# A residue layout for the rows of the compressed keys and values, an immediate factor in GpSimd's rounding product, and GpSimd's loops written out

## What is computed

```python
def compress(k, pos, w1, w2):
    B, G, T, dh = k.shape
    c = k.reshape(B, G, T // CMP_STRIDE, CMP_STRIDE, dh)
    blocks = jnp.concatenate([c[:, :, :-1], c[:, :, 1:]], axis=3) + pos
    flat = blocks.reshape(B, G, blocks.shape[2], CMP_BLK * dh)
    return jax.nn.gelu(flat @ w1) @ w2
...
    kc = compress(to_g(partial_rope(kv(nkc), cos, sin)), cmp_pos_k, cmp_w1_k, cmp_w2_k)
    vc = compress(to_g(kv(nvc)), cmp_pos_v, cmp_w1_v, cmp_w2_v)
```

## Time and profile before

| | us |
|---|---|
| median of three runs | 3132.75 |
| lowest, highest run | 3125.09, 3135.55 |
| the profiled execution | 3136.32 |
| its span, from the first to the last instruction | 3134.3 |

### The profile page before, as it was taken

The page is one execution under the profiler, slowest core; times in us unless marked ns, Lnnn a source line. Parts: engine busy times, 40 slices in busy tenths (PEclk is TensorE's granted clock), DMA queues, the critical chain, the costliest instruction groups (busy, mean ns, idle before and its releaser), DMA issues.

```text
span 3134.3 us, 41325 instructions
## 1 busy us (share of the span) xinstructions
PE 3074.6 (98%) x15116; PEld 2466.4 (79%) x15116; DVE 1501.1 (48%) x2613; ACT 724.1 (23%) x1461; POOL 1902.8 (61%) x885
## 2 busy tenths in 40 slices
PE   8999999999999999999999999999999999999998
PEld 6688888868888888877688888888887668888887
DVE  4654520455552143886645455214388664545411
ACT  4410100441100123434601110012343550111000
POOL 4277778437777876001288777787700128877776
PEclk9999999999999999999999999999999999999999
DMA  3132333213333322112033333332211203233222
GB/s 124 48 108 98 97 95 100 75 34 108 101 94 95 100 87 88 48 35 81 21 94 94 101 99 95 95 100 88 87 48 35 81 22 100 94 101 94 100 94 87
DMA packets 71713, 262.29 MB, mean 84 GB/s; under 512 B 8208, under 2 KB 8208, under 8 KB 71440
## 3 DMA queue, kind: packets, MB, share of 16 engines
q1 hardware_dynamic: 71280, 258.34, 25.9%
q10 hardware_dynamic: 288, 1.98, 0.2%
HBM read 258.20 MB, written 2.10 MB: 83 GB/s over the span
## 4 chain that ended last, share of the span: by engine, by line
PE 85%; DVE 6%; issue 4%; POOL 3%; ACT 2%; DMA 0%; DVEq 0%; POOLq 0%; SPq 0%; ACTq 0%
PE bank L642 83%; POOL w_hi L1408 1%; POOL w_lo L1416 1%; PE bank L1272 1%; DVE arena L1983 1%; DVE bank L1983 1%; DVE rope L1983 1%; PE bank L657 0%; DVE arena L2354 0%; DVE rope L1980 0%; ACT act_hi L1563 0%; ACT arena L1905 0%; DVE w_lo L2380 0%; DVE x L1983 0%; ACT bank L1562 0%
## 5 line engine op out<-in xcount | busy, mean ns | idle before, releaser
L1408 POOL TENSOR_TENSOR w_hi<-ring,one 128x1024 fp32r<-128x1024 f32 x430 | 818.7, 1904 | 1160.9 <-PE bank L642 578.4
L1416 POOL TENSOR_TENSOR w_lo<-ring,w_hi 128x1024 fp32r<-128x1024 f32 x422 | 1039.0, 2462 | 40.3 <-DVE h_lo L2007 7.5
L642 PE MATMUL bank<-h_hi,w_hi 128*128 128x512 f32 x2256 | 893.9, 396 | 3.4 <-POOL w_lo L1416 3.4
L642 PE MATMUL bank<-h_hi,w_lo 128*128 128x512 f32 x2256 | 879.6, 390 | 0.0
L642 PE MATMUL bank<-h_lo,w_hi 128*128 128x512 f32 x2256 | 879.0, 390 | 0.0
L642 PE MATMUL bank<-act_hi,w_hi 128*128 128x512 f32 (+1 forms) x1376 | 507.2, 395 | 6.1 <-POOL w_lo L1416 2.7
L642 PEld LDWEIGHTS bank<-h_hi,w_hi 128*128 128x128 f32 x2256 | 423.1, 188 | 97.0 <-issue 5.4
L642 PEld LDWEIGHTS bank<-h_hi,w_lo 128*128 128x128 f32 x2256 | 423.0, 187 | 90.9
L642 PEld LDWEIGHTS bank<-h_lo,w_hi 128*128 128x128 f32 x2256 | 423.4, 188 | 84.9 <-issue 1.0
L642 PE MATMUL bank<-act_hi,w_lo 128*128 (+1 forms) x1120 | 438.2, 391 | 0.0
L642 PE MATMUL bank<-act_lo,w_hi 128*128 (+1 forms) x1120 | 420.9, 390 | 1.4 <-DVE act_lo L2574 1.4
(11 more groups left out here) (248 smaller groups left out, 2863.6 us busy)
## 6 DMA issues: line engine op xcount, KB each, us to landing
ring<-wstream SPq DMA_DIRECT2D x480, 512.0 KB, 3.5
par<-params SPq DMA_DIRECT2D x4, 529.5 KB, 4.3
x<-xT SPq DMA_DIRECT2D x4, 512.0 KB, 7.2
outT<-h SPq DMA_DIRECT2D x4, 512.0 KB, 2.7
cst<-const ACTq DMA_DIRECT2D x1, 1412.0 KB, 8.9
par<-params ACTq DMA_DIRECT2D x1, 525.5 KB, 5.2
arena<-pos SPq DMA_DIRECT2D x1, 256.0 KB, 2.6
cst<-const SPq DMA_DIRECT2D x1, 24.5 KB, 2.4
```

The lines of the kernel that those rows point to most:

```text
L642: return pe.matmul(out, lhsT, rhs, start=start, stop=stop)
L1408: return po.tensor_tensor(out, a, one.broadcast_to([P, n]), ALU.mult)
L1416: po.tensor_tensor(pair_[1], raw, pair_[0].bitcast(F32), ALU.subtract).then_inc(done.sem, 1)
```

## The change

- GpSimd's `times_one` becomes `rounded`: the product of the tile with an immediate number 1.0 (`tensor_scalar`), one tensor input in place of two. The tile `one`, its memset and its semaphore go.
- GpSimd's loops over layers and tiles are written out, so its waits are for constants.
- The rows `ck` and `cv` are laid out by residue: token 16b+r stands in column 32r+b. `hidden` then reads 31 neighbouring columns of each of three rows. ScalarE's copy of `nvc` and the two products of `rope(0)` write in that order, the shift by one token becomes a shift by NB = 32 columns (480 columns instead of 511), and the bias columns move accordingly.

```diff
-                                       data[:, :, 2 * p:2 * p + 16 * (NCMP - 1) + 1:16], p == 0, p == 15)
+                        at = p % 8 * 2 * (T // 16) + p // 8
+                                       data[:, :, at:at + NCMP], p == 0, p == 15)
...
-            def times_one(out, a, n):
-                return po.tensor_tensor(out, a, one.broadcast_to([P, n]), ALU.mult)
+            def rounded(out, a):
+                return po.tensor_scalar(out, a, 1.0, None, ALU.mult)
...
-                with po.Fori(0, 7) as it:
+                for it in range(0, 7):
...
-                with po.Fori(0, 3) as it:
+                for it in range(0, 3):
...
-            po.memset(one[:, :], 1.0).then_inc(s_one, 1)
-            po.wait_ge(s_one, 1)
-            with po.Fori(0, LAYERS) as l:
+            for l in range(0, LAYERS):
                 mixer1(l)
                 ffn(l, l, 0, MIX1_TILES, PER1)
-            with po.Fori(0, LAYERS) as l:
+            for l in range(0, LAYERS):
                 mixer2(l)
                 ffn(l, l + LAYERS, BASE2, MIX2_TILES, PER2)
...
-                        last = sc.activation(dst, b[:, :], ACT.Copy)
+                        if name == "nvc":
+                            last = sc.activation(by_residue(dst), by_token(b[:, :]), ACT.Copy)
+                        else:
+                            last = sc.activation(dst, b[:, :], ACT.Copy)
...
-                ve.tensor_copy(cv[64:P, 0, 0:T - 1], cv[0:64, 0, 1:T]).then_inc(cv_o.sem, 1)
+                ve.tensor_copy(cv[64:P, 0, 0:T - NB], cv[0:64, 0, NB:T]).then_inc(cv_o.sem, 1)
...
-                    mul(ropes, rotation_bank(i)[:, :], C("sin2")).then_inc(rp_p.sem, 1)
-                    mul(ropec, raw_block(i), C("cos2")).then_inc(rp_p.sem, 1)
+                    if i == 0:
+                        mul(by_residue(ropes), by_token(rotation_bank(0)[:, :]), by_token(C("sin2"))).then_inc(rp_p.sem, 1)
+                        mul(by_residue(ropec), by_token(raw_block(0)), by_token(C("cos2"))).then_inc(rp_p.sem, 1)
...
-                        d = 1 if i == 0 else 0
+                        d = NB if i == 0 else 0
```

More of the change, by code:

```diff
@@ L123, in build @@
         w_lo = sb("w_lo", [P, 2, TILE], F32R)
-        one = sb("one", [P, 1])
         bank = [ctx.enter_context(nc.psum_tensor(f"bank{i}", [P, T], F32)) for i in range(8)]
@@ L266, in build @@
         s_pos = ctx.enter_context(nc.semaphore("positions_and_columns_loaded"))
-        s_one = ctx.enter_context(nc.semaphore("one_laid"))
         s_par = signal("params_loaded", 16)
@@ L446, in build, with by_residue, by_token @@
         LIN_PLACED = {hd: 10 * (hd + 1) for hd in range(4)} | {4: 59, 5: 60, 6: 79, 7: 80}
+        def by_residue(a):
+            return a.rearrange("p (r b) -> p b r", r=16)
+        def by_token(a):
+            return a.rearrange("p (b r) -> p b r", r=16)
         def raw_block(i):
@@ L1405, in _ @@
         def _(po):
-            def times_one(out, a, n):
-                return po.tensor_tensor(out, a, one.broadcast_to([P, n]), ALU.mult)
+            def rounded(out, a):
+                return po.tensor_scalar(out, a, 1.0, None, ALU.mult)
             def halves(raw, pair_, high, count, done, clear=None):
-                times_one(pair_[0], raw, TILE).then_inc(high.sem, 1)
+                rounded(pair_[0], raw).then_inc(high.sem, 1)
                 po.wait_ge(high.sem, count)
@@ L1439, in mixer1 @@
                             c = slice(n * TILE // 2, (n + 1) * TILE // 2)
-                            times_one(early[0][0][:, c], ring[:, 0, c], TILE // 2).then_inc(w1_h.sem, 1)
+                            rounded(early[0][0][:, c], ring[:, 0, c]).then_inc(w1_h.sem, 1)
                             po.wait_ge(*w1_h(l, n))
@@ L1506, in split @@
                             c = slice(n * TILE // 2, (n + 1) * TILE // 2)
-                            times_one(w_hi[:, w, c], raw[:, c], TILE // 2).then_inc(w_h.sem, 1)
+                            rounded(w_hi[:, w, c], raw[:, c]).then_inc(w_h.sem, 1)
                             po.wait_ge(*w_h(nf, FFN_TILES + n))
@@ L2430, in mixer2, with bias_columns, bias_rows @@
                 ck, cv = m2["ck"], m2["cv"]
+                NB = T // 16
+                def bias_columns(a):
+                    return a[:, 2, :].rearrange("p (a b) -> p a b", b=2 * NB)[:, :, 0:2]
+                def bias_rows(name):
+                    return par[:, PAR2[name]].rearrange("p (two a) -> p a two", two=2)
                 ve.tensor_copy(cv[0:64, 1, :], cv[64:P, 0, :]).then_inc(cv_o.sem, 1)
                 ve.wait_ge(*cv_o(l, 1))
-                ve.tensor_copy(cv[64:P, 0, 0:T - 1], cv[0:64, 0, 1:T]).then_inc(cv_o.sem, 1)
-                ve.tensor_copy(cv[64:P, 1, 0:T - 1], cv[0:64, 1, 1:T]).then_inc(cv_o.sem, 1)
-                ve.tensor_copy(cv[:, 2, 0:32:2], par[:, PAR2["pos_v"]]).then_inc(cv_o.sem, 1)
-                ve.tensor_copy(ck[:, 2, 0:32:2], par[:, PAR2["pos_k"]]).then_inc(cv_o.sem, 1)
+                ve.tensor_copy(cv[64:P, 0, 0:T - NB], cv[0:64, 0, NB:T]).then_inc(cv_o.sem, 1)
+                ve.tensor_copy(cv[64:P, 1, 0:T - NB], cv[0:64, 1, NB:T]).then_inc(cv_o.sem, 1)
+                ve.tensor_copy(bias_columns(cv), bias_rows("pos_v")).then_inc(cv_o.sem, 1)
+                ve.tensor_copy(bias_columns(ck), bias_rows("pos_k")).then_inc(cv_o.sem, 1)
                 ve.memset(m2["hid"][:, 124:126], 0.0).then_inc(cv_o.sem, 1)
@@ L2442, in rope @@
                         ve.wait_ge(*rp_o(l, (4, 5, 6, 7, 8, 12)[i - 1]))
-                    mul(ropes, rotation_bank(i)[:, :], C("sin2")).then_inc(rp_p.sem, 1)
-                    mul(ropec, raw_block(i), C("cos2")).then_inc(rp_p.sem, 1)
+                    if i == 0:
+                        mul(by_residue(ropes), by_token(rotation_bank(0)[:, :]), by_token(C("sin2"))).then_inc(rp_p.sem, 1)
+                        mul(by_residue(ropec), by_token(raw_block(0)), by_token(C("cos2"))).then_inc(rp_p.sem, 1)
+                    else:
+                        mul(ropes, rotation_bank(i)[:, :], C("sin2")).then_inc(rp_p.sem, 1)
+                        mul(ropec, raw_block(i), C("cos2")).then_inc(rp_p.sem, 1)
                     ve.wait_ge(*rp_p(l, 2 * i + 2))
```

## The result

The changed kernel takes 3203.4 us (median of six runs, 3198.1 to 3210.3) where the kernel before takes 3134.4 us in the six runs beside it. The ratio is 1.0217, its 95% interval 1.0200 to 1.0233. The profiled execution took 3203.43 us, with a span of 3201.6 us. The forecast of 3120.5 us missed, and the measured time lies outside its range; the case called "slower" in the prediction is the one that came true.

What follows compares the result with a forecast made beforehand. TensorE was taken as the bound, busy 3074.6 of 3134.3 us. Savings of 6.8 (compression) and 5.5 us (shorter high parts), 12.3 in all, took 3132.75 to 3120.5 us; range 3110 to 3131.

Steps and rivals of the forecast that it cites:

- slower: Rival, every tile: GpSimd becomes the bound above 2.5 us (`w_out`, merge) or 2.8 (nets); 3.0 gives near 3250 us; chance 0.08.
- The price of the immediate product: GpSimd's high part of 1024 columns, one input in place of two: 1.4 us, bounds 1.0 and 2.4.
- x: Time saved per GpSimd high part by the one-input product: 0.5 us taken, 0.9 and -0.5 as ends.
- the steady stretches: Tiles where GpSimd waits 1.02 us (feed-forward) or 0.74 us (`w_out`) for TensorE: x worth nothing, no loss at -0.5.
- The compression's matmuls: Four hidden blocks reading neighbouring columns: step 0.161 to 0.108 us, block 5.33 to 3.63; 6.8 us saved.
- The layout's writes: ScalarE's copy and VectorE's two products in 128-byte steps: at most doubled, 0.6 and 1.4 us, covered, so costed at nothing.
- The loops: GpSimd's written-out loops: 0 taken; bounds 0.1 us gained at each of eight late places, or a few us of fetch stall.
- Items 1 to 5: Places where TensorE waits and a shorter high part helps: start, `w_out`, net starts, linear attention, sums of squares; 5.5 us.
- items 2 and 3: The first block's two `w_out`, 1.0 us gained, and the four starts of the feed-forward net, 2.0 us, at x 0.5.
- Item 5: Sums of squares at the second block's start, held beside GpSimd's low part: 1.2 us gained.
- items 3 and 4: Four feed-forward starts, 2.0 us, and mixer2's linear attention twice, 1.0 us: VectorE's two-input instructions stand still while GpSimd reads.
- The clock: Dips of a few us in TensorE's granted clock may come or go: 2 us either way each, only widening the range.

Runs made afterwards that it cites:

- e7: Against e4, GpSimd's high parts use the single immediate product in the four feed-forward nets only: 51.2 us above e4, ratio to the kernel before 1.0154.
- e8: Against e4, GpSimd's high parts use the single immediate product in the mixers only, nets two-input: 18.5 us above e4, ratio to the kernel before 1.0046.
- e11: Against e4, every GpSimd high part is a product with 1.0 plus addition of 0.0 in one instruction: 3120.0 us, ratio to the kernel before 0.9937.
- e12: Against e4, every GpSimd high part is a plain rounding copy: ratio to the kernel before 0.9942.
- e4: Kernel before plus residue layout and written-out GpSimd loops, two-input product kept: 3132.2 us, ratio to the kernel before 0.9991.

## Why the prediction was wrong

**The price of the immediate product.** This is the step that failed. It was taken at 1.4 us with bounds of 1.0 and 2.4, and is 2.77 us in a steady tile, 2.80 on average. The argument ran: a real second stream costs 2.4, a repeated one 1.89, so none costs 1.4. But these two rows are the same kind of instruction with two inputs, and the changed one is another kind; nothing in the trace of before was of it. The upper bound failed for the same reason: that a general routine costs no more than a subtraction was an assumption, not a row. That one input can be fast, as the same text argued from ScalarE's 1.24 us, is true (1.04 and 1.05 us in the fast forms), only not in this form. So x, put at +0.5, was 1.89 - 2.77 = -0.88 us, and with it fell the sentence that the steady stretches hold: more is used than the 2.51 - 1.89 = 0.62 us that a tile really has free in the nets.

**The free time.** The slower rival was right in its mechanism and its place ("every tile"), and wrong in two sizes. Some 0.1 us was taken off for the handing over; the trace has 0.32 from TensorE's last matmul to GpSimd's start, and 0.13 from the low part to the first matmul. So the nets tip at 2.51 us, not at 2.8, and by the text's own points a product of 2.77 would have cost nothing there; they lost 51 us. That hand-over is the first wrong size. The second is the loss by place: with 2.77 us the text's rule gives nothing in the nets and (2.77 - 2.53) x 158 = 38 us in the rest, and e7 and e8 measured 51.2 and 18.5. For 3.0 us it gave 53 us in the nets and 73 in the rest. The cycle's sum gives 264 x (0.32 + 3.0 + 0.08 + 2.40 + 0.13 + 5.54 - 10.88)/2 = 78 for the nets. Its chance of 0.08 rested on "nothing in the trace suggests it", while nothing in the trace spoke of this instruction's price at all, so it was far too low.

**The compression's matmuls.** Right: 6.3 us of matmul time, 6.7 at equal clock, forecast 6.8. The step from record to record was forecast at 0.108; 3.71 us a block give (3.71 - 0.28)/31 = 0.111, the upper end of what was read from the earlier trace rows.

**The layout's writes.** Right that they cost nothing. They became longer by 1.5 to 1.75 times, within the bound of two, and lie where it was said.

**The loops.** Taken at 0; measured about 2 us, within the bound that the text gave; two waits show it, its cause is open.

**Items 1 to 5, the waits that a shorter high part would cut.** With the price of the instruction as assumed they cannot be judged by the changed kernel, but e11 and e12 do judge them. With x = 0.86 these kernels gained 10.3 and 12.2 us against e4 where the sum gave 8.6. The first four places were right: the start of the kernel gave 0.7 us where 0.5 was forecast, the waits for low parts of items 2 and 3 gave 4.8 where it was 5.1, with the first net's start as described (0.83 to 0.17), and `rope` 2.1 where it was 1.8. Item 5 was wrong: the waits at the two sums of squares grew, by 1.1 us together, where 1.2 us of gain were counted. That the total still came out near is in part luck, since 4.6 us of it lie where no row shows them. The reading behind items 3 and 4, that the one-input product still blocks VectorE for a shorter time, held for the fast forms (0.9 of 1.06 us). It did not hold for the immediate product of the changed kernel, which blocks for its first 0.9 us and leaves VectorE alone for the other 1.9.

**One-input work on GpSimd.** Of the two statements of the Trainium skill (GPSIMD Engine Reference, Engine selection and the cycle accounting) the first, that one-input work is roughly line rate, is nearer to the fast forms: 1024 elements in 1.04 us. The 1.8 cycles an element as the best case, an estimate of 1.54 us in the prediction, is beaten by them. Neither fits the immediate product, which takes 2.77 us.

**The clock.** The 2 us either way were meant for single dips that move when work shifts; no run here isolates one. Between single runs of one kernel the spread is larger, some 3 us for each 0.001 of mean clock. It had next to no part in the result: 0.993 in the profiled run of before and 0.992 in that of after, which is 2.9 us of 67.

## What to carry to other kernels

Price an instruction by a row of its own kind, and where there is none, run it alone first; fewer inputs is no argument. A GpSimd rounding pass as a plain copy or with two immediate operations takes 1.05 us for 1024 columns, as a single operation 2.8, with two inputs 1.9. An engine that fills two buffers for another has free time only after both hand-overs are taken off, here 0.45 us a tile, and when it runs out, look for the loss in the spacing of the starts and in the length of the chain's pieces, not in the idle time.

## What the hardware showed that was not expected

- GpSimd, fp32 to fp32r, 128x1024, one tensor input: copy 1.04, product and sum with immediates 1.05, product with an immediate 2.77, product with a column 2.86 us; two inputs: product with a repeated column 1.90, subtraction 2.40 us.
- A one-input instruction of GpSimd holds VectorE's two-input instructions for its first 0.85 to 0.9 us, whether it lasts 1.06 or 2.77 us. Beside the rest of the immediate product they run undisturbed (0.41 and 0.69 us); beside a two-input instruction they stand still (2.57 and 2.67 us).
- The other way round, a two-input product of GpSimd that starts while a two-input instruction of VectorE runs took 2.34 us in place of 1.89.
- A stall of TensorE of 0.13 us leaves no idle time in the records, and the matmul after it is followed 0.10 us late. Over the kernel some 60 us, nearly all of them stalls, were booked as busy time.
- TensorE reading fp32 columns 64 bytes apart takes 0.161 us a record, neighbouring ones 0.111 us. Writes in steps of 128 bytes took ScalarE 1.05 us in place of 0.60 and VectorE 1.04 to 1.10 in place of 0.68.
